# Three chained transformer blocks on one core: second layer's conditioning summed on VectorE, and the even layer's 31-tap convolution on TensorE

## The reference, cut to what matters

```
m  = silu(c) @ ada_w[i] + ada_b[i]          # six vectors of 1024 for each layer i = 0, 1
h += m[2] * mixer(modulate(rms_norm(h), m[0], m[1]))
h += m[5] * ec_moe(modulate(rms_norm(h), m[3], m[4]))
```

## Time and profile before

| | |
|---|---|
| median of 3 runs | 2328.44 us (2328.24 to 2328.85) |
| the profiled execution's own time | 2325.14 us |
| its span, first to last instruction | 2322.9 us |
| PE busy | 1960.7 us (84%) |
| PEld busy | 1153.0 us (50%) |
| DVE busy | 594.2 us (26%) |
| ACT busy | 290.4 us (13%) |
| POOL busy | 131.7 us (6%) |
| mean granted PE clock | 0.929 of full speed |
| moved by DMA | 634.48 MB, 273 GB/s over the span |

### The profile page before, as it was taken

How to read it: one execution, slowest core, us unless ns; L and a number is a source line. 1 busy time by engine, 2 the same in 40 slices (tenths; PEclk the granted TensorE clock), 3 DMA queues, 4 the chain that set the end, 5 groups by cost and what they waited for, 6 DMA issues and landing times.

```text
span 2322.9 us, 30376 instructions
## 1 busy us (share of the span) xinstructions
PE 1960.7 (84%) x12649; PEld 1153.0 (50%) x12649; DVE 594.2 (26%) x1686; ACT 290.4 (13%) x750; POOL 131.7 (6%) x177
## 2 busy tenths in 40 slices
PE   8999999899655566699966556669999999999999
PEld 4455556555322222387532223224568854548874
DVE  1323337712000000122210000004625411334430
ACT  1023411431000000010200000001500001300000
POOL 0200006400000000000000000002100000010000
PEclk9999999899888887899997887879999999999999
DMA  9658347839999999975899999999234444324420
GB/s 365 250 187 318 128 163 256 324 116 382 425 426 427 427 426 427 388 228 217 333 425 426 426 427 425 427 422 336 73 110 145 155 147 151 109 73 146 163 107 18
DMA packets 191439, 634.48 MB, mean 273 GB/s; under 512 B 6529, under 2 KB 90641, under 8 KB 158840
## 3 DMA queue, kind: packets, MB, share of 16 engines
q1 hardware_dynamic: 186912, 623.79, 69.2%
q0 software_dynamic: 1504, 5.83, 0.7%
q10 hardware_dynamic: 2936, 3.66, 0.4%
HBM read 632.15 MB, written 1.09 MB: 273 GB/s over the span
## 4 chain that ended last, share of the span: by engine, by line
PE 64%; DMA 32%; DVE 2%; ACT 1%; issue 1%; POOL 0%; SPq 0%; DVEq 0%; ACTq 0%
DMA ring<-in_moe_w_down 32%; PE bank L647 17%; PE bank L662 17%; PE bank L2573 7%; PE bank L2050 4%; PE bank L999 3%; PE bank L747 2%; PE bank L713 1%; PE bank L950 1%; PE bank L738 1%; PE bank L2225 1%; PE bank L2034 1%; PE bank L1952 1%; PE bank L2529 1%; DVE arena L1487 1%; PE bank L561 1%
## 5 line engine op out<-in xcount | busy, mean ns | idle before, releaser
L2034 PE MATMUL bank<-ring,arena 128*32 128x256 f32 x3968 | 303.0, 461 | 185.9 <-DMA ring<-in_moe_w_up 113.2
L2034 PEld LDWEIGHTS bank<-ring,arena 128*32 128x32 f32 x3968 | 138.8, 128 | 336.6 <-DMA ring<-in_moe_w_up 147.3
L647 PE MATMUL bank<-ring,hT 128*128 128x512 f32 (+2 forms) x704 | 299.1, 583 | 5.0 <-DVE hT L2213 2.9
L662 PE MATMUL bank<-xn,ring 128*128 128x256 f32 x1280 | 276.6, 379 | 0.0
L662 PEld LDWEIGHTS bank<-xn,ring 128*128 128x128 f32 x1280 | 243.2, 190 | 33.0
L2050 PE MATMUL bank<-ring,arena 128*32 128x256 f32 x1984 | 162.7, 485 | 76.9 <-DMA ring<-in_moe_w_down 66.9
L647 PEld LDWEIGHTS bank<-ring,hT 128*128 128x128 f32 x704 | 133.6, 192 | 157.3 <-issue 153.8
L2573 PE MATMUL bank<-ring,arena 128*128 128x512 f32 x352 | 151.6, 592 | 0.0
L2050 PEld LDWEIGHTS bank<-ring,arena 128*32 128x32 f32 x1984 | 73.2, 134 | 154.5 <-DMA ring<-in_moe_w_down 83.4
L1843 DVE TENSOR_TENSOR arena<-arena,bank 128x256 f32<-128x256 f32 x32 | 13.5, 421 | 495.2 <-ACT arena L1904 495.2
L662 PE MATMUL bank<-hT,ring 128*128 128x256 f32 x512 | 111.3, 379 | 1.3 <-ACT arena L1357 1.3
(11 more groups left out here) (409 smaller groups left out, 1837.8 us busy)
## 6 DMA issues: line engine op xcount, KB each, us to landing
ring<-in_moe_w_gate SPq DMA_DIRECT2D x62, 2048.0 KB, 26.5
ring<-in_moe_w_up SPq DMA_DIRECT2D x62, 2048.0 KB, 26.0
ring<-in_moe_w_down SPq DMA_DIRECT2D x62, 2048.0 KB, 26.1
ring<-in_ada_w SPq DMA_DIRECT2D x24, 2048.0 KB, 11.7
ring<-in_w_up SPq DMA_DIRECT2D x44, 1024.0 KB, 7.6
ring<-in_w_in SPq DMA_DIRECT2D x11, 2048.0 KB, 17.5
ring<-in_w_down SPq DMA_DIRECT2D x10, 2048.0 KB, 7.8
ring<-in_w_out SPq DMA_DIRECT2D x6, 2048.0 KB, 22.3
```

The lines of the kernel that those rows point to most:

```text
L647: ins = t_.matmul(bank[b][:, 0:n], lhsT(k)[:, P * t:P * t + P], w[:, k, c0:c0 + n], start=(k == 0), stop=(k == kt - 1))
L662: ins = t_.matmul(bank[b][:, 256 * (j % 2):256 * (j % 2) + 256], w[:, k, P * j:P * j + P], rhs[:, k, :], start=(k == 0), stop=(k == 7), sk ...
L2034: ins = t_.matmul(bank[4][32 * j:32 * j + 32, at:at + 256], xs_now[b][:, 4 * (c % 2) + k, :], w(k)[:, 256 * j:256 * j + 256], start=(c % 2 ...
```

## The change

Three things are changed.

1. Layer 1's conditioning is no longer multiplied by PE. DVE sums each piece: eight operations of 128x512, each a row block of the piece times silu(c) of that block, added up (`ada_sums_dve`). This leaves 128 partial rows per piece. Four pieces at a time, PE adds the partitions up with a stationary operand of 32 columns of ones on four strips (`ada_fold_pe`), ACT copies, PE turns (`ada_turn_pe`), and DVE adds the bias. The twelve pieces move to block 1: seven among the projections, one after branch a, two after branch b, two after `out1_0`. DVE releases their ring slots.
2. The convolution is done by PE. For each channel tile, the gated channels are copied by DMA inside SBUF into four groups of 32 channels, each four times with a shift of 0 to 3 tokens, so that the 128 partitions hold 32 channels by 4 taps. A tile is then 8 groups of taps by 4 groups of channels, 32 matmuls of 128x32x256. POOL builds the stationary operands (tap weights times a folded identity). The DMAs of tiles 0 and 1 are issued by ACT after `glu0` (16), those of tiles 2 and 3 by POOL (16 each). The matmuls run beside steps 0 to 3 and 5 to 8 of `b2`. DVE adds the bias from the bank.
3. The convolution's bank is taken from the scores: `b2` uses two banks (`TWO`). The layer norm's sums start one step later.

Cut to its core:

```diff
+ADA_BY_DVE = {"in0": 1, "in1": 1, "cmp_v": 1, "in4": 1, "in6": 1, "in2": 1, "in3": 1, "branch_a": 1, "branch_b": 2, "out1_0": 2}
+ADA_BATCHES = ((0, 1, 2, 3), (6, 7, 8, 9), (4, 5, 10, 11))
...
+        def ada_sums_dve(*turns):
+            v = nc.vector
+            v.wait_ge(*act_s.after("c silu"))
+            for n in turns:
+                name = f"ada1_{ADA_BY_DVE_ORDER[n]}"
+                await_chunk(v, name)
+                if n >= 6:
+                    v.wait_ge(*pe_s.after(("ada1.turn0" if n == 9 else f"ada1.fold{(n - 6) // 4}")))
+                w, acc = slot(name), ada_sum[:, n % 6, :]
+                for k in range(8):
+                    if k == 0:
+                        ins = v.tensor_scalar(acc, w[:, k, :], c_silu[:, k:k + 1], None, ALU.mult)
+                    else:
+                        v.wait_ge(*dve_s.latest())
+                        ins = v.scalar_tensor_tensor(out=acc, in0=w[:, k, :], scalar=c_silu[:, k:k + 1], in1=acc, op0=ALU.mult, op1=ALU.add)
+                    ins.then_inc(*dve_s.signals(*([f"used {name}"] if k == 7 else [])))
+        def ada_fold_pe(m):
+            claim(FOLD_BANK)
+            t_.wait_ge(*dve_s.after(f"used ada1_{ADA_BATCHES[m][3]}"))
+            for j in range(4):
+                ins = t_.matmul(bank[FOLD_BANK][32 * j:32 * j + 32, :], constant("one").to_broadcast([P, 32]), ada_sum[:, (4 * m + j) % 6, :],
+                                start=True, stop=True, skip_group_check=True)
+        def ada_turn_pe(m):
+            t_.wait_ge(*act_s.after(f"ada1.rows{m}"))
+            for b in range(4):
+                features = slice(b, 512, 4) if m == 1 else slice(P * b, P * b + P)
+                ins = t_.matmul(bank[FOLD_BANK][:, 4 * b:4 * b + 4], ada_rows_of(m)[:, features], ident[:, 0:P:32],
+                                start=True, stop=True, skip_group_check=True)
...                                               # block1_dve, in its order
+            ada_sums_dve(0)                       # ahead of the copy of in0
+            ada_sums_dve(1)                       # ahead of the copy of in1
+            ada_sums_dve(2, 3)                    # ahead of the copy of in4
+            ada_sums_dve(4)                       # ahead of the copy of in6
+            ada_sums_dve(5)                       # ahead of the copy of in2
+            ada_turn_dve(0)
+            ada_sums_dve(6)                       # ahead of the copy of in3
+            ada_sums_dve(7)                       # ahead of branch a
+                    ada_sums_dve(8)               # ahead of the context norm, between branches a and b
+            ada_turn_dve(1)                       # ahead of the copies of the context turn
+            ada_sums_dve(9)
-            residual_dve("out1_0", 0)
+            residual_dve("out1_0", 0, after=lambda t: ada_sums_dve(10 + t))
...                                               # even_pe
-                for c in itertools.islice(pieces, ADA_EVEN[i]):
-                    ada_rows_pe(c)
+                if i == 0:
+                    ada_turn_pe(2)
             dense_pe("ev_q", own, by=(act_s, act_s))
-            for c in pieces:
-                ada_rows_pe(c)
...
+        CONV_AT = {0: (0, 0), 1: (0, 1), 2: (1, 0), 3: (1, 1), 5: (2, 0), 6: (2, 1), 7: (3, 0), 8: (3, 1)}
+            def conv31_pe(k, half):
+                if half == 0:
+                    if k % 2 == 0:
+                        claim(CONV_BANK)
+                    t_.wait_ge(s_shift[max(0, k - 1)], 16 * 16)
+                    waits(t_, (pool_s, f"tap weights{k}"))
+                for g in range(4 * half, 4 * half + 4):
+                    for q in range(4):
+                        ins = t_.matmul(bank[CONV_BANK][32 * q:32 * q + 32, S * (k % 2):S * (k % 2) + S], tap_w[k][:, q, g, :],
+                                        shifted[k][:, q, 4 * g:4 * g + S], start=(g == 0), stop=(g == 7), skip_group_check=True)
-            attention_pe("b2", units2, before=turned("kx", kx_items) + turned("qx", qx_items), also=beside_b2)
+            attention_pe("b2", units2, before=turned("kx", kx_items) + turned("qx", qx_items), also=beside_b2, scores=TWO)
...                                               # even_act, after the sigmoid of glu0
+                    for j, q in itertools.product(range(4), range(4)):
+                        a.dma_start(shifted01[32 * j:32 * j + 32, :, q, 0:SHIFTED], glu[32 * q:32 * q + 32, 0:2, j:j + SHIFTED]).then_inc(s_shift[0], 16)
...                                               # even_pool
-            conv31_pool(range(0, 15))
+            waits(g, (pe_s, "hx.T3"), (pe_s, "ada1.turn1"))
+            tap_weights_pool([0, 3])
+            g.wait_ge(*pe_s.after("ada1.fold2"))
+            tap_weights_pool([1])
             for t in range(2):
                 rstd_pool("ev_q_g", *[b[:, 8 * t:8 * t + 8] for b in q_ss], HD, tile=t)
-                if t == 0:
-                    conv31_pool(range(15, 18))
-            conv31_pool(range(18, CONF_K))
+            g.wait_ge(*pe_s.after("ada1.turn2"))
+            tap_weights_pool([2])
+            waits(g, (dve_s, "glu1"), (pe_s, "ev_q.acc1"))
+            shift_pool(2)
+            waits(g, (pe_s, "hm0.T3"))
+            shift_pool(3)
+        def tap_weights_pool(tiles):
+            for k in tiles:
+                w = col("ev_conv_w_2", 32 * k, 32).rearrange("p (q g) -> p q g", g=8)
+                for q in range(4):
+                    ins = nc.gpsimd.tensor_tensor(tap_w[k][:, q], constant("fold").unsqueeze(1).to_broadcast([P, 8, 32]),
+                                                  w[:, q].unsqueeze(2).to_broadcast([P, 8, 32]), ALU.mult)
+        def shift_pool(k):
+            for j, q in itertools.product(range(4), range(4)):
+                nc.gpsimd.dma_start(shifted[k][32 * j:32 * j + 32, q, 0:SHIFTED], glu[32 * q:32 * q + 32, k, j:j + SHIFTED]).then_inc(s_shift[k - 1], 16)
```

More of the change, by code:

```diff
@@ L222, in weight_chunks, with conditioning, by_dve @@
     w_in = A["w_in"][0]
-    ada = iter([(f"ada{l}_{i}", l, i) for l in range(2) for i in range(12)])
-    def conditioning(n=1):
-        for _ in range(n):
-            name, l, i = next(ada)
+    ada = [iter([(f"ada{l}_{i}", l, i) for i in order]) for l, order in enumerate((range(12), ADA_BY_DVE_ORDER))]
+    def conditioning(layer, n):
+        for name, l, i in itertools.islice(ada[layer], n):
             whole(name, A["ada_w_2"][l], 0, 8, 512 * i, 512 * i + 512)
+    def by_dve(name):
+        conditioning(1, ADA_BY_DVE[name])
     for i in IN_ORDER:
         whole(f"in{i}", w_in, 0, 8, 512 * i, min(512 * i + 512, 3864))
-        conditioning(ADA_AFTER_IN.get(i, 0))
+        conditioning(0, ADA_AFTER_IN.get(i, 0))
+        if f"in{i}" in ADA_BY_DVE:
+            by_dve(f"in{i}")
         if i == 1:
@@ new lines, in ada_fold_act @@
+        def ada_fold_act(m):
+            nc.scalar.wait_ge(*pe_s.after(f"ada1.fold{m}"))
+            nc.scalar.activation(ada_rows_of(m), bank[FOLD_BANK][:, :], ACT.Copy).then_inc(*act_s.signals(f"ada1.rows{m}"))
+        def ada_turn_pe(m):
+            t_ = nc.tensor
+            claim(FOLD_BANK)
+            t_.wait_ge(*act_s.after(f"ada1.rows{m}"))
[3 more added lines that the diff above has]
+                                start=True, stop=True, skip_group_check=True)
+            ins.then_inc(*pe_s.signals(f"ada1.turn{m}"))
+            lend(FOLD_BANK, (dve_s, f"ada1.m{m}"))
@@ new lines, in ada_turn_dve @@
+        def ada_turn_dve(m):
+            nc.vector.wait_ge(*pe_s.after(f"ada1.turn{m}"))
+            for half in range(2):
+                i = ADA_BATCHES[m][2 * half]
+                dst = mod[:, 1].rearrange("p v k c -> p (v k) c")[:, 4 * i:4 * i + 8, 0].rearrange("p (j b) -> p j b", b=4)
+                src = bank[FOLD_BANK][:, 0:16].rearrange("p (b j) -> p j b", j=4)[:, 2 * half:2 * half + 2]
+                nc.vector.tensor_tensor(dst, src, col("ada_b_2", 48 + 4 * i, 8).rearrange("p (j b) -> p j b", b=4), ALU.add)\
+                    .then_inc(*dve_s.signals(*([f"ada1.m{m}"] if half else [])))
@@ L1015, in beside_pe @@
                 ada_rows_pe(ADA_STEPS[step])
-            for l, at in ADA_LAST.items():
-                if step == at + 2:
-                    ada_columns_pe(l)
+            if step == ADA_LAST + 2:
+                ada_columns_pe()
         def beside_act(step):
@@ L1265, in block1_pe @@
             project_and_condition(6)
+            ada_fold_pe(0)
             claim(7)
```

200 lines of the change are left out of this document (95 added, 105 removed), and 2 rows, old and new, of the table COLS.

## The result

| | before | after |
|---|---|---|
| median of 12 runs each | 2326.99 us | 2331.23 us |
| the profiled execution's own time | 2325.14 us | 2331.24 us |
| its span | 2322.9 us | 2329.4 us |

The ratio of the times is 1.0021, with a 95% interval of 1.0011 to 1.0031. A gain of 7.3 us was forecast as the likeliest; the kernel became about 4 us slower. The number lies inside the range (2313 to 2333), but on the other side of no change.

A forecast was written before the change was run, and what follows sets the result against it. PE was taken to bound the kernel before the first expert, at 532 us, and DMA after it. Terms 6.1 - 8.0 - 7.0 + 1.6 = -7.3 took the median 2328.44 to 2321.1 us; range 2313 to 2333.

The forecast's parts named there:

- the landing of in4: Block 1 projections: in4's load lands at 65.9, PE wants it at 63.64; +2.3 us, bounds 0 and 4.
- the branches: Block 1 up to the out projection: DVE's sum before the context norm and PE's fold and turn 1 side by side; +2.0 us.
- Fold and turn 0: Block 1 projections: PE's added four-matmul fold and four-matmul turn of the conditioning; +1.8 us.
- No further wait: Projections after in4: later chunks land in time; the seventh sum ends at 131, 2 us ahead of the qb turn's copy.
- rival A: Loads starve the projections: seventh piece lands at 132.5, DVE finishes at 138; 5.5 us more, 0.6 at in4; 2327; chance 0.2.
- A wait for DVE ahead of the context turn: Block 1 branches: a sign, named beforehand, that would show the prediction wrong; no size given.
- Even layer: Up to attention b2: two pairs of pieces go -7.1, fold and turn 2 +1.8, third pair -2.7; -8.0 us.
- b2: -7.0 + 1.6: Attention b2 with the convolution: less idle time and slow clock, -7.0 (bounds -3 and -10); wait for tile 3, +1.6.
- the 1.6 for tile 3: b2, step 7: POOL's DMAs at 0.70 each land tile 3 at E+32.9, PE wants it at E+31.3; bounds 0 and 16.
- the layer norm's 1-column matmuls: b2: they should lower PE's clock once more, as at 466; 1.6 us of loss kept within the -7.0.
- The clock of b2 near 0.66: b2: a granted clock staying near 0.66 was named beforehand as a sign of the prediction being wrong.
- Rival C: b2 gives only 3 us: two banks bind in every pair and the clock falls as before; 2325; chance 0.1.

The follow-up runs named there:

- after_again: The kernel after once more, unchanged, for a second profile and more times: 2331.3 us, ratio 1.0033 to the kernel before.
- order_in4: Kernel after with in4's load seventh in the queue instead of ninth, DVE summing pieces 1 to 3 ahead of its in4 copy: 2336.8 us.
- spread_three: Kernel after with three score banks, in4 seventh in the queue, two early summed pieces and the second and third folds and turns moved later: 2336.5 us.
- turn1_late: Kernel after with the second conditioning turn placed behind the context and merged-row turns on PE and DVE: 2329.9 us.
- wide_sums: Kernel after with the layer norm's sums of squares as products of 128x64 instead of 128x1: 2324.8 us, ratio 0.9994 to the kernel before.
- before_wide: Kernel before with its sums of squares as products of 128x64 instead of 128x1: 2324.4 us, ratio 0.9988 to the kernel before.
- three_banks: Kernel after with b2's scores on three banks again and the convolution in a bank of its own: 2326.1 us, ratio 0.9999 to the kernel before.
- fill_waits: Kernel after with three unused 128x128x256 products at each of b2's steps 9 and 11, where PE waited: 2329.9 us.

## Why the prediction was wrong

Two large terms of its sum were wrong, the landing of in4 and the clock in b2, and a smaller one, the branches. The rest held in size, in part by luck.

**Block 1, in4: +2.3 forecast, 8.4 measured.** The landing was put at 65.9 by adding one chunk of 5.4 to the 22.2 MB of the earlier trace rows; in4 landed at 70.3. The stretch up to 60.5 moved 359 GB/s, not 367, and by 70.3 the engines had moved 21.7 + 9.8 x 0.387 = 25.5 MB, 1.2 more than the queue up to in4 holds: chunks issued behind it had their share (argued from the count, not tested). Of the 4.4 us that in4 landed late, the 0.5 MB less by 60.5 are 1.3, and the 1.2 MB of others 3.1. Then the wait of 5.40 cost a second time: in4 took 17.04 instead of 14.00 at the lower clock. This second price wasn't in the sum at all. The wait alone is outside the bounds of 0 and 4. after_again agrees: 5.48, and 16.54 for in4.

**Fold and turn 0: +1.8, measured 1.06 + 1.05 less overlap, 1.7.** Right. "No further wait" came true by luck. The sum was to find the seventh piece landed at 125.4 and to end at 131; it started at 132.38 and ended at 138.3, within 0.3 of what rival A said (132.5 and 138). PE didn't wait for it because in4 had already made PE itself 8.4 late. order_in4, which removes that wait, ran into DVE's queue at once, and spread_three too. The price of rival A was thus there behind the wait at in4.

**The branches: +2.0, measured 3.6.** A sum is 5.95, not 5.4, and turn 1 was priced as lying beside DVE's work. It holds a bank until DVE's two small operations, which stand behind the last merged tile; PE's context turn can't start before (0.98 in the row of 319.64), and takes 3.77. turn1_late gave 0.96 of it back. A wait for DVE ahead of the context turn was one of the prediction's signs of being wrong. The remaining 2.7 of the 16.5 at out1 were not in the sum: the first 32 records of transposes took 6.45 instead of 5.14, and b1 was 1.4 longer, with a granted clock of 0.83 from 230 to 250 us. Neither is tied to the change by a run; after_again has out1 at 320.1.

**Even layer: -8.0, measured -8.4** (99.83 instead of 108.28 from out1 to b2, in both profiles of the kernel after). Up to the end of ev_q the removed pairs with the fold and turn gave 5.5 for 5.3, and attention started 8.9 after it for 9.0.

**b2: -7.0 + 1.6, measured -0.1.** Of the work, two banks cost the two waits of 0.61 (0.55 forecast). POOL's issues were 0.50, below the bound of 0.54, and the 1.6 for tile 3 fell away. wide_sums has b2 at 57.5, near the 57.0 forecast ahead of tile 3, but not for the reasons given: the 57.0 contain 1.6 for the fall behind the one-column products, which wide_sums hasn't, and lack the 1.5 of slow clock at b2's start, which it has. What failed is the step "the layer norm's 1-column matmuls should lower the clock once more as they did at 466: 1.6". The mechanism was the right one; the size was taken from a place where the clock had come back after 3.4 us (before_wide confirms 1.6 there). In the kernel after it stays down almost to the end of b2, and costs 6.4. Why the clock comes back after 3.4 us in one kernel and after 14 in the other is open. The clock of b2 near 0.66 was another sign of being wrong, and the stretch from 465 to 480 has 0.64. Rival C had the outcome, b2 giving little, but not the cause: two banks bind at two steps, not in every pair, and wide_sums has both waits and no fall there.

With the terms at their measured size the sum of the prediction is 6.1 + 6.1 (in4) + 1.6 (branches) - 8.4 - 0.1 = +5.3. With the 2.7 of lower clock ahead of out1 it is 8.0 at ev_out (7.9 measured), and less the 1.6 that come back in ev_out 6.4 at the first expert (6.3). The median is 4.2 higher. The prediction's parts for "faster" (0.42, 0.11 and 0.06) add up to 0.59, not 0.58.

## What to carry to other kernels

A reduction that needs one column can be tried with 64: here the products took the same time to 0.05 us, and the clock behind them stayed up. Work moved to an idle engine must be placed in that engine's own queue, between what it waits for and what others wait for from it; its free time as a share says nothing, and a load put ahead of one that is nearly late costs its wait and the slow clock behind the wait. A forecast of a clock loss has bounds from nothing to the rest of the stage, not the one size that a trace shows.

## What the runs showed of the hardware that was not expected

- Sixteen records of products of 128x1 took 1.95 us and sixteen of 128x64 2.00, at the full clock. During the first or within 2 us behind them the granted clock fell to the level of 1.2 GHz in nine of eleven profiles (all but three_banks and fill_waits), for 3 to 14 us; behind the second, up to the end of b2, in none of three. PE was never idle for more than 0.61 us at a time in the 15 us ahead of them. The Trainium skill, TensorE: Matmul & The Clock Gate, section HAM oscillation, puts a fall down to gaps in which PE is idle; for this fall the traces don't agree, as the edit that removed it left the gaps alone. The falls at ev_out's start, behind an idle 2.87, are of the kind it tells of, but the kernel after and before_wide had the same 2.87 and no fall.
- An issue of a small DMA inside SBUF took 0.50 us on POOL's queue (35.5 KB) and 0.84 on ACT's (71 KB, so the two are not compared like with like).
- A 128x512 operation of DVE with a per-partition scalar and a sum, each waiting for the one before, takes 0.78 from one to the next; the product and sum of this size had shown 0.72.
- The same code, from block 3's first transpose to the end, took 751.3 to 755.4 us in the fourteen profiles, so a single profile can't tell 4 us, 0.2%.
